# RWKV's gate units moved from the preparation into the attention's rounds, and a triangle solver that takes two pairs of heads at once

## The reference

```
xn = rms_norm(h, norm_w)
p = xn @ w_in                                   # 1024 x 8320 columns
p_tm = p[:, :3200]; p_tm += (shift(p_tm) - p_tm) * mu_shift
r, k, v, w_lo, a_lo = split(p_tm)               # 16 heads of 64
gate = p[:, 3200:4224]                          # RWKV's gate
y_rwkv = (group_norm(rwkv7(r, k, v, ...)) + bonus) * silu(gate)
y_att = dilated_attention(p[:, 4224:7296], 3 patterns) * silu(p[:, 7296:8320])
h = h + concat(y_rwkv, y_att) @ w_out
```

## Time and profile before

| what | us |
|---|---|
| median of 3 runs | 3044.23 (3044.05 to 3054.51) |
| span of the profiled execution | 3047.4 |
| attention rounds 1 to 6, each | 66.7 |
| last attention round | 59.0 |
| TensorE busy | 2825.7 |

### The profile page before, as it was taken

The page is one execution under the profiler, slowest core; times in us unless marked ns, Lnnn a source line. Parts: engine busy times, 40 slices in busy tenths (PEclk is TensorE's granted clock), DMA queues, the critical chain, the costliest instruction groups (busy, mean ns, idle before and its releaser), DMA issues. The chain is left out here.

```text
span 3047.4 us, 52649 instructions
## 1 busy us (share of the span) xinstructions
PE 2825.7 (93%) x21272; PEld 2206.7 (72%) x21272; DVE 1653.7 (54%) x3101; ACT 1255.6 (41%) x2310; POOL 361.1 (12%) x525
## 2 busy tenths in 40 slices
PE   8999999989998999999999999996887899989998
PEld 6666777766676777776777777775777777778776
DVE  3555665732357534556565555474466664652565
ACT  4344443221224445555554433443344334532234
POOL 0000000000000011111110056675340000000000
PEclk9988999999998999999999999998989999999999
DMA  3000111242224542323333335337534454421114
GB/s 116 28 14 22 42 42 36 73 158 70 69 80 131 162 145 65 78 72 78 79 81 86 112 134 165 125 124 279 169 98 145 150 199 140 152 81 49 35 62 152
DMA packets 187073, 312.39 MB, mean 103 GB/s; under 512 B 78144, under 2 KB 119376, under 8 KB 185296
## 3 DMA queue, kind: packets, MB, share of 16 engines
q1 hardware_dynamic: 186832, 309.04, 32.3%
HBM read 237.10 MB, written 71.89 MB: 101 GB/s over the span
## 5 line engine op out<-in xcount | busy, mean ns | idle before, releaser
L255 PE MATMUL ps<-xs,wparts 128*128 128x512 f32 x1664 | 698.6, 420 | 11.9 <-DVE xs L1515 9.3
L257 PE MATMUL ps<-xs,wparts 128*128 128x512 f32 x1664 | 655.0, 394 | 0.0
L256 PE MATMUL ps<-xs,wparts 128*128 128x512 f32 x1664 | 654.8, 393 | 0.0
L323 DVE TENSOR_TENSOR wparts<-wring,wparts 128x1024 fp32r<-128x1024 f32 x248 | 305.8, 1233 | 316.8 <-ACT wparts L315 292.9
L255 PEld LDWEIGHTS ps<-xs,wparts 128*128 128x128 f32 x1664 | 313.7, 189 | 130.9 <-issue 68.0
L315 ACT ACTIVATE wparts<-wring 128x1024 fp32r<-128x1024 f32 x248 | 263.0, 1061 | 275.3 <-PE ps L257 213.1
L257 PEld LDWEIGHTS ps<-xs,wparts 128*128 128x128 f32 x1664 | 313.5, 188 | 71.8
L256 PEld LDWEIGHTS ps<-xs,wparts 128*128 128x128 f32 x1664 | 314.4, 189 | 60.6 <-issue 4.8
L2269 POOL COPY perm<-qkg 128x1024 f32<-128x1024 f32 x32 | 63.1, 2008 | 1511.7 <-ACT qkg L359 1115.1
L2415 ACT ACTIVATE Pm<-Pm,ml 128x128 f32<-128x128 f32 (+1 forms) x384 | 168.0, 440 | 140.5 <-DVE ml L2483 140.4
L2483 DVE CUSTOM_DVE_ANT_0 Pm<-ps,mask 128x128 f32<-128x128 f32 (+1 forms) x384 | 110.9, 349 | 187.6 <-PE ps L2318 187.6
(11 more groups left out here) (408 smaller groups left out, 4868.3 us busy)
## 6 DMA issues: line engine op xcount, KB each, us to landing
wring<-in_wo SPq DMA_DIRECT2D x96, 512.0 KB, 3.5
ops<-rw SPq DMA_DIRECT2D x32, 640.0 KB, 6.1
wring<-in_w SPq DMA_DIRECT2D x39, 512.0 KB, 3.6
wring<-in_w2u SPq DMA_DIRECT2D x33, 512.0 KB, 4.4
wring<-in_wg SPq DMA_DIRECT2D x24, 512.0 KB, 3.6
wring<-in_w2v SPq DMA_DIRECT2D x24, 512.0 KB, 3.9
wring<-in_w2a SPq DMA_DIRECT2D x24, 512.0 KB, 6.6
MB<-wst SPq DMA_DIRECT2D x48, 256.0 KB, 5.0
```

The costliest lines, as they stand in the source:

```text
L255: nc.tensor.matmul(out, a, c, start=start, stop=False)
L256: nc.tensor.matmul(out, b, c, start=False, stop=False)
L257: return nc.tensor.matmul(out, a, d, start=False, stop=stop)
L323: K.nc.vector.tensor_tensor(W.part(i, 1), W.raw(i), W.part(i, 0).bitcast(F32), ALU.subtract).then_inc(*K.dve.done("w_lo", W.first + i))
```

## The change

Three things change together.

1. The eight gate units of RWKV leave the preparation. Pair p's unit now runs in the attention's round p, as the fourth unit of the round, behind the attention's own gate unit; the units are paced at six steps in seven (32 steps stretched over 37 of 39). In the last round the fill is three units at two steps in three. The result goes to a new buffer `rg` and by a new transfer `rg_store` into the same place of `rw`. `prep_store` has five transfers.
2. The units of r, k and v that are left: four behind the attention (r, k, v of pair 0 and r of pair 1), then 3, 3, 3, 3, 3, 2, 2 and 1 in the preparation's rounds. In the last round the triangles of pair 7 and the first stage of the recurrence start 17 steps into the round (`later(17, ...)`), beside the rest of the small work.
3. The solver works on 128 partitions, two pairs at once, four times in all. Its transfers move in rounds 2, 4 and 6, and for pairs 6 and 7 at the start of the recurrence.

```
-    order, sizes = iter([(p, x) for p in range(1, NP) for x in range(4)]), [4] * 5 + [3, 3, 2]
+BEHIND, PASSES, LAST_AT = [(0, 0), (0, 1), (0, 2), (1, 0)], [3] * 5 + [2, 2, 1], 17
+    order = iter([(p, x) for p in range(NP) for x in range(3)][len(BEHIND):])
...
 def prep_sp(K, A, B):
+    first = [1 + len(BEHIND) + sum(PASSES[:p]) for p in range(NP)]
     for p in range(NP):
-        for i in range(4 * p + 3 if p else 6, 4 * p + 7):
...
+        for at in (first[p] + 3, first[p] + 4, first[p] + 5):
+            while i <= min(at, 24):
+                yield from w_load(K, B.W, i)
+                i += 1
+            if at == first[p] + 3 and p:
+                yield from mb_store(K, A, B, p - 1)
+            if at == first[p] + 4 and p in (2, 4, 6):
+                yield from solve_move(K, A, B, p // 2 - 1)
+        if p < NP - 1:
+            yield from prep_store(K, A, B, p)
-    yield from mb_store(K, A, B, NP - 2)
     yield from rwkv_first_sp(K, A, B.rw)
...
 def solve_pool(K, B, j):
-    G = B.G[0:64, :].rearrange("p (i t) -> p i t", t=32)
+    G = B.G[:, :].rearrange("p (i t) -> p i t", t=32)
...
 def prep_pe(K, A, B):
-        yield from weave(in_turn(*[prep_unit_pe(K, B, *u) for u in units],
-                                 *([triangles_pe(K, B, p), rwkv_first_pe(K, B.rw, B.RU)] if p == NP - 1 else [])),
-                         prep_small_pe(K, B, p), *([triangles_pe(K, B, p - 1)] if p else []))
+        yield from weave(in_turn(*[prep_unit_pe(K, B, *u) for u in units]),
+                         *([later(LAST_AT, in_turn(triangles_pe(K, B, p), rwkv_first_pe(K, B.rw, B.RU)))]
+                           if p == NP - 1 else []), prep_small_pe(K, B, p), *([triangles_pe(K, B, p - 1)] if p else []))
...
 def att_sp(K, A, B):
-        for i in range(3 * p + 4, 3 * p + 7):
+        for i in range(4 * p + 4, 4 * p + 8):
             if p < 7:
                 yield from w_load(K, B.W, i)
-            if p and i == 3 * p + 4:
+            if p and i == 4 * p + 4:
+                yield from rg_store(K, A, B, p - 1)
                 yield from weights_move(K, A, B, p - 1)
...
+def rg_store(K, A, B, p):
+    K.sp.wait_ge(*(yield "uev", ATT_W0 + att_unit(p, 3), 1))
+    K.nc.sync.dma_start(A["rw"][p][:, 6144:7168], B.rg).then_inc(*K.sp.done("rg_store", p, by=16))
...
-                         units(K, B, p + 1) if p < 7 else paced(fill(K, B), 1, 2))
+                         paced(units(K, B, p + 1), 6, 7) if p < 7 else paced(fill(K, B), 2, 3))
...
 def rwkv_sp(K, A, B):
-    yield from solve_move(K, A, B.prep, NP - 2)
+    yield from solve_move(K, A, B.prep, NP // 2 - 1)
...
         if n == 6:
-            yield from solve_move(K, A, B.prep, NP - 1)
-        if n == 9:
-            yield from xt_store(K, A, B.prep, NP - 1)
-            K.sp.wait_ge(*(yield "xt_store", NP - 1))
+            yield from xt_store(K, A, B.prep, NP // 2 - 1)
+            K.sp.wait_ge(*(yield "xt_store", NP // 2 - 1))
             yield from mix_load(K, A, B, 15)
```

More of the change, by code:

```diff
@@ L1635, in prep_layout @@
     B.mbs = early[:, 1, 160:928].rearrange("p (c x) -> p c x", x=192)
-    last = [x[:, 0, 0:768].rearrange("p (c x) -> p c x", x=192) for x in (B.v, B.gate, B.Kc, B.bon)]
+    last = [x[:, 0, 0:768].rearrange("p (c x) -> p c x", x=192) for x in (B.v, B.spare, B.Kc, B.bon)]
     B.stage = lambda p, q: last[q] if p == NP - 1 else B.mbs
@@ L1686, in prep_early_sp @@
 def prep_early_sp(K, A, B):
-    for i in (1, 2):
+    for i in range(3):
         yield from w_load(K, B.W, i)
@@ L1743, in solve_move, with xt_store @@
[L1743 to L1756, removed]
+def xt_store(K, A, B, j):
+    K.sp.wait_ge(*(yield "solved", j))
+    for p in (2 * j, 2 * j + 1):
+        for i, here, there in corners(A, B, p, 128):
+            K.nc.sync.dma_start(there, here).then_inc(
+                *K.sp.done("xt_part", p, i, by=16, also=[("xt_store", j)] if p % 2 and i == 3 else []))
@@ L1759, in solve_pool, with solve_move @@
+def solve_move(K, A, B, j):
+    for p in (2 * j, 2 * j + 1):
+        K.sp.wait_ge(*(yield "mb_store", p, 3))
+    if j:
+        yield from xt_store(K, A, B, j - 1)
+        K.sp.wait_ge(*(yield "xt_store", j - 1))
+    for p in (2 * j, 2 * j + 1):
+        for i, here, there in corners(A, B, p, 0):
+            K.nc.sync.dma_start(here, there).then_inc(
+                *K.sp.done("g_part", p, i, by=16, also=[("g_load", j)] if p % 2 and i == 3 else []))
+def solve_pool(K, B, j):
     nc, pool = K.nc, K.pool
-    G = B.G[0:64, :].rearrange("p (i t) -> p i t", t=32)
@@ L1801, in prep_behind_pe @@
     B.RU = at.RU.join(at.RS)
-    yield from prep_units_pe(K, B, 0)
-def prep_units_pe(K, B, p):
-    for x in range(4):
-        yield from prep_unit_pe(K, B, p, x)
+    for u in BEHIND:
+        yield from prep_unit_pe(K, B, *u)
 def prep_unit_pe(K, B, p, x):
-    yield from unit_pe(K, B.W, prep_unit(p, x), B.xs, B.xkeys, B.RU, "shift" if x < 3 else "uev")
+    yield from unit_pe(K, B.W, prep_unit(p, x), B.xs, B.xkeys, B.RU, "shift")
     yield STEP
@@ L1932, in prep_act @@
     for p, units in enumerate(prep_groups()):
-        yield from weave(in_turn(*[prep_unit_act(K, B, *u) for u in units],
-                                 *([rwkv_first_act(K, B.rw)] if p == NP - 1 else [])), prep_small_act(K, B, p))
+        yield from weave(in_turn(*[prep_unit_act(K, B, *u) for u in units]),
+                         *([later(LAST_AT + 12, rwkv_first_act(K, B.rw))] if p == NP - 1 else []), prep_small_act(K, B, p))
     barrier(K, act, 3)
@@ L2076, in prep_dve @@
     for p, units in enumerate(prep_groups()):
-        yield from weave(in_turn(*[prep_unit_dve(K, B, *u) for u in units],
-                                 *([triangles_dve(K, B, p), rwkv_first_dve(K, B.rw)] if p == NP - 1 else [])),
-                         prep_small_dve(K, B, p), *([triangles_dve(K, B, p - 1)] if p else []))
+        yield from weave(in_turn(*[prep_unit_dve(K, B, *u) for u in units]),
+                         *([later(LAST_AT, in_turn(triangles_dve(K, B, p), rwkv_first_dve(K, B.rw)))]
+                           if p == NP - 1 else []), prep_small_dve(K, B, p), *([triangles_dve(K, B, p - 1)] if p else []))
     barrier(K, dve, 3)
@@ L2089, in prep_pool @@
     nc.gpsimd.memset(B.mbs[:, :, 128:192], 0.0).then_inc(*pool.done("mb_zero"))
-    for p in range(NP):
-        yield from solve_pool(K, B, p)
+    for j in range(NP // 2):
+        yield from solve_pool(K, B, j)
 def att_layout(K, A, st, xs, W, b1):
@@ L2193, in att_sp @@
         yield from w_load(K, B.prep.W, i)
+    yield from rg_store(K, A, B, 7)
     yield from att_store(K, A, B, 7)
+    sp.wait_ge(*(yield "rg_store", 7))
     sp.wait_ge(*(yield "att_store", 6))
```

105 lines of the change are left out of this document (49 added, 56 removed).

## The result

The changed kernel takes 3034.0 us (median of 20 runs, 3023.0 to 3046.1); the kernel before, in as many runs beside it, 3045.6. The ratio is 0.9962, with a 95% interval of 0.9952 to 0.9973: 11.5 us (0.38%) faster, with 8 to 15 in the interval. That is a difference the runs can tell from none, and it is inside the 0.5% that I had named as no change. The forecast was 3028, 16 us under its base of 3044.2.

A forecast was written before the change was run, and what follows sets the result against it. TensorE, busy 2825.7 of 3047.4 us, was taken as the bound, so only its idle time could be gained. 61 - 54.5 - 16 - 4 - 2.5 = -16 gave 3031, or 3028 as median; range 3009 to 3049.

The forecast's parts named there:

- Attention, rounds 0 to 6: Each round gains a unit of 10.9 us, which fills 3.45 us of TensorE's idle time: 7.85 a round, +55.
- the 0.4 for changes between shapes: In each attention round, 0.4 us added for more changes between matmul shapes.
- Last round: Last attention round: one unit more, idle time filled, 2 us for late preparation loads; +6, between +4 and +14.
- Table loads: Attention, ScalarE: another pair of table loads a round, 2.6 us, costed at nothing; 18 us in seven rounds if exposed.
- Preparation: Rounds 0 to 4 lose a unit each, -54.5; rounds 5 to 7 take 114 us against 130, -16.
- Into the recurrence: Behind the preparation: 0.5 MB less gate traffic and stores and loads 2.7 us earlier; -4, between 0 and -11.
- Solver: GpSimd: instructions on 128 partitions cost the same as on 64; recurrence -2.5 us, between 0 and -5.
- (1): Whole kernel: the forecast itself holds, 3020 to 3036 us; chance 0.45.
- (2): Preparation: rounds 5 and 6 covered at 33.4 us, -9, and the recurrence starts 7 earlier: 3012; chance 0.17.
- (3): Attention: idle time stays or table loads are exposed; half to all of 24 us returns: 3040 to 3052; chance 0.26.
- (4): Preparation: VectorE's chain decides from 44.3 us a round, TensorE pauses and its clock falls; 48 us slower, 3076; chance 0.12.

The follow-up runs named there:

- e3: The changed kernel with the four units of an attention round one step per step, not six in seven: 3036.5 us, ratio 0.9970.
- e1: The changed kernel with the last attention pair's final multiply ahead of the fourth unit's shift on VectorE, not behind it: 3033.1 us, ratio 0.9946.
- e4: The changed kernel with both Silu gates of the attention's rounds made plain copies: 3035.0 us, ratio 0.9966.
- e6: The kernel before with only the new solver, two pairs at once on 128 partitions; gate units stay in the preparation: 3036.5 us, ratio 0.9979.
- e2: The changed kernel with the old solver, one pair at a time on 64 partitions; gate units stay moved: 3084.3 us, ratio 1.0130.
- e12: The changed kernel with early loads, early multiply, three units behind the attention and the third solve in the recurrence: 3022.9 us, ratio 0.9918.

## Why the forecast came out as it did

The range (3009 to 3049) held the time, and 3034 lies in the case I held likeliest (3020 to 3036). The point was 6 us too low: 4.5 by the difference, -16 for a measured -11.5, and the rest by the base, 3044.2 for 3045.6. That was enough to turn a small gain that I called faster, at 0.45, into one that is the same, at 0.43. The stretch alone was forecast at -13.5 and measured -9.5. Its parts miss by -1.3 (attention, rounds 0 to 6), +3.0 (last round and what stands behind it), +2.9 (preparation) and -0.8 (into the recurrence); the rest is rounding. By steps:

**Attention, rounds 0 to 6, +55.** Right. From the first row maximum of round 0 to that of round 7 it is 465.9 us before and 519.6 after, +53.7. Rounds 1 to 6 cost 7.4 or 7.5 more each, forecast 7.85: the 0.4 for changes between shapes was not there. Round 0, 65.3 us before, costs 8.9 more. The reason given for it, that unit steps fill the bare part, is right; that the spreading is needed, which I took from the change, is not (e3).

**Last round, +6, and nothing behind it.** Here a step failed. I priced the late loads inside the round (+2) and took the four units behind the attention as four units either way. The exchange of a gate unit for one with a shift put a wait of VectorE ahead of `att_out`, and with it ahead of the barrier: TensorE waits 8.1 us at L1827 where it waited 2.2. The prediction should have asked what stands behind the new shift on VectorE. From the last round's first row maximum to `kk0` of pair 0 the kernel before takes 107.4 us and the change 116.4, +9.0 for the forecast +6. In e1 it is 112.3, +4.9. So this step cost 4.1 us at that place and 3.3 of the stretch, less than the 5.9 by which the wait grew.

**Table loads at nothing.** Right, and shown by e4.

**Preparation, -54.5 and -16.** Rounds of three at 44.3, as forecast: from the first `kk0` to the first mask of round 5 it is -54.2. From there to the last `Bc` the kernel before takes 129.8 us and the change 116.4, -13.4 for -16. The rounds of pairs 5 and 6, from mask to mask, take 40.9 and 38.9 us against 39.4 and 36.2: 4.2 us over. Round 5 has its solve beside it and waits of 3.7 and 2.4 us of VectorE for triangle stores to land, where I had left one of 4.6; round 6 begins with 5.2 us in which VectorE waits for the sigmoid behind TensorE. The granted clock, 0.91 and 0.94 there, had no term in my sum; no run separates its share. Round 7 came out as forecast: 40.4 us from its mask to `Bc` before and 36.6 after, -3.8, and 42.4 to 38.6 was -3.8 too. The 38.6 counts from TensorE's triangle, 1.1 us ahead of the mask, and I had set it against a 41.3 that starts at `kk0`: by its own terms the sum of the three was -16.8. The new solver alone takes 5.0 off that round (36.3 for 41.3 in e6, from `kk0`).

**Into the recurrence, -4.** Measured -4.8.

**Solver.** The price per partition was right: a sum takes 662 ns on 128 partitions, 635 on 64; a product 634 (599 on 64).

```profile
L1776 POOL TENSOR_TENSOR solve<-solve,step 128x30 f32<-128x30 f32 (+14 forms) x120 | 79.4, 662 | 9.4
L1772 POOL TENSOR_TENSOR step<-solve 128x30 f32<-128x30 f32 (+14 forms) x120 | 76.1, 634 | 9.4
```

A solve of two pairs takes 46.6 us from its first to its last instruction (1967.28 to 2013.86) where one pair took 43.7. The solves beside the preparation differ among themselves: 40 to 48 us for the six before, 44 to 48 for the three after. What it is worth was misread. I booked it as a wait of 13.3 us that goes and a gain of 2.5 in the recurrence. The first is there, 4.2 us alone. The second no profile settles: the recurrence took 328.1 us before and 322.7 in e6, with the new solver alone, but 330.4 in the change and 327.4 in e2, with the old one. And the main thing was missing: that the old solver's cycle, 51 to 58 us in e2, is longer than the new rounds, so that the move is worth -5 with the new solver and +36 without (e2, e6). The rows for it were at hand, a solve of 43.7, a round of 44.3 and the wait of 13.3. This did not move the forecast, as both halves came together.

**The rivals.** (1) is the outcome. (2) is excluded: rounds 5 and 6 were not covered; with another split of the units and the solve moved, e12 gets 10.5 us of the stretch. (3) is excluded in both halves: the attention's idle time went, and the table loads are hidden. (4) did not come: rounds of three show no wait at all. The side it ends on is real, though, by another chain: with the old solver the kernel is 38 us slower.

## What to carry to other kernels

When rounds are shortened, list every engine's and queue's cycle per round, not only the bound engine's: a helper that fitted a round of 55 us became the bound at 44. When a piece of work is exchanged for another of the same kind, look at what is queued behind it on the engines that do its small parts; here a shift in place of nothing held a barrier. And where a load is named as the last releaser and was issued behind a barrier, look at what else stands behind the same barrier before you move the load alone: here that gained nothing, and an earlier barrier gained 3 us.

## What was not expected of the hardware

GpSimd's operations on 128 partitions take 4 to 6% more than on 64, for twice the work. These are means over solves with different work beside them; at the start of the recurrence the solve takes 34.5 us on 64 and 35.9 on 128, 4% more. The Trainium skill (GPSIMD Engine Reference, 2. Architecture) gives each of its eight cores 16 partitions; with 64 in use half of them would stand, and the rows agree.

The same recurrence took 325.8 to 330.8 us in seven profiles that do not differ in it. The granted clock dips in other places each time. In the sixth stretch of 40 us it is 0.77 in the change and 0.93 in e3. A term below 5 us in that stage cannot be read from one profile of each kernel; the way from the first statistics store to the first `kk0`, where the change's clock is 1.00 up to 1690 us and 0.98 behind it, took 574.9 to 575.8 us in the five kernels that leave it alone or touch only its table loads.
